# A decoder trunk with expert retrieval: PE's 16 products ahead of its step of mixing in every turn

## The reference

```
h = rms_norm(x, norm_mix);  z = h @ w_in                 # 1024 -> 2564
mixed = [forgetting attention | dilated attention | differential attention | S5 scan with GLU]
x = x + mixed @ w_out
h = rms_norm(x, norm_ffn)
# PEER: 8 heads, each with 2 x 128 keys; q = h @ peer_wq
top 16 of each half, top 16 of the 256 sums, gate = softmax(best 16)
act = gelu(sum_d h[t,d] * u_tab[id]) * gate              # 128 experts a token
x = x + sum_k act[t,k] * v_tab[id]
```

## Time and profile before

| | |
|---|---|
| median of 3 runs | 1836.1 us |
| the profiled execution | 1842.02 us |
| its span, first to last instruction | 1839.1 us |
| granted TensorE clock, mean | 0.905 |
| busy: PE / DVE / POOL / ACT | 1493.1 / 1157.0 / 1082.8 / 389.9 us |
| products of rows of v (L1112) | 2048 instructions, 982.4 us busy, 636 ns each |
| dot products (L865) | 512, 627.4 us busy, 1225 ns each |
| moved by DMA | 649.87 MB, of which 536.94 MB are gathers |

### The profile page before, as it was taken

The page is one execution under the profiler, slowest core; times in us unless marked ns, Lnnn a source line. Parts: engine busy times, 40 slices in busy tenths (PEclk is TensorE's granted clock), DMA queues, the critical chain, the costliest instruction groups (busy, mean ns, idle before and its releaser), DMA issues.

```text
span 1839.1 us, 15963 instructions
## 1 busy us (share of the span) xinstructions
PE 1493.1 (81%) x4780; PEld 799.9 (43%) x4780; DVE 1157.0 (63%) x2646; ACT 389.9 (21%) x991; POOL 1082.8 (59%) x1028
## 2 busy tenths in 40 slices
PE   6758379889898589889998579879998778777777
PEld 3546235445474234445464234445455433232332
DVE  6644954867469943877468933876648965445453
ACT  2221012233221121233221111233221121111111
POOL 0000345767666655777666655666766667777774
PEclk9768789989998889988999889999998988999889
DMA  7415589989999999999999999999999989999997
GB/s 307 160 35 207 204 359 380 399 297 363 373 401 408 340 418 409 405 369 385 374 401 408 336 415 351 395 340 331 374 376 405 369 301 410 409 409 409 407 388 307
DMA packets 179053, 649.87 MB, mean 353 GB/s; under 512 B 17783, under 2 KB 19319, under 8 KB 174105
## 3 DMA queue, kind: packets, MB, share of 16 engines
q0 software_dynamic: 147456, 536.94, 76.0%
q1 hardware_dynamic: 31512, 111.92, 15.7%
HBM read 644.07 MB, written 4.72 MB: 353 GB/s over the span
## 4 chain that ended last, share of the span: by engine, by line
PE 41%; DVE 32%; DMA 13%; issue 8%; POOL 4%; ACT 2%; DVEq 0%; SPq 0%; POOLq 0%
PE ps L1112 21%; DVE junk L865 12%; DMA ring_u<-table_u,ids 11%; PE ps L934 8%; PE ps L1069 3%; POOL ring_v L1143 2%; PE ps L1082 2%; DMA ring_v<-table_v,ids 1%; PE ps L999 1%; POOL ring_u L1138 1%; DVE W L690 1%; DVE W L842 1%; DVE W L844 1%; DVE W L845 1%; PE ps L1009 1%
## 5 line engine op out<-in xcount | busy, mean ns | idle before, releaser
L1112 PE MATMUL ps<-ring_v,diag 128*128 128x512 f32 x2048 | 982.4, 636 | 229.2 <-ACT diag L480 227.6
L865 DVE CUSTOM_DVE_ANT_0 junk<-ring_u,h 128x1024 bf16<-128x1024 f32 x512 | 627.4, 1225 | 268.1 <-DMA ring_u<-table_u,ids 212.5
L1138 POOL DMA_INDIRECT ring_u<-table_u,ids x512 | 536.1, 1047 | 387.7 <-DVE ids L849 204.9
L1143 POOL DMA_INDIRECT ring_v<-table_v,ids x512 | 546.5, 1067 | 352.2 <-PE ps L1112 269.9
L1112 PEld LDWEIGHTS ps<-ring_v,diag 128*128 128x128 f32 x2048 | 412.0, 205 | 761.4 <-issue 751.6
L471 ACT ACTIVATE acts<-dots 128x4 f32<-128x4 f32 x128 | 26.3, 205 | 998.6 <-DVE dots L865 998.6
L480 ACT ACTIVATE diag<-cst,weights 128x128 f32<-128x128 f32 x512 | 163.5, 390 | 39.2 <-DVE weights L874 39.0
L934 PE MATMUL ps<-W,hT 128*128 128x384 f32 (+2 forms) x384 | 142.9, 531 | 4.0 <-DVE hT L576 2.6
L1082 PE MATMUL ps<-hT,W 128*128 128x128 f32 x1024 | 117.7, 276 | 2.7 <-DVE hT L576 2.6
L1082 PEld LDWEIGHTS ps<-hT,W 128*128 128x128 f32 x1024 | 116.0, 192 | 3.8 <-DVE hT L576 3.8
L934 PEld LDWEIGHTS ps<-W,hT 128*128 128x128 f32 x384 | 73.7, 193 | 72.3 <-issue 36.9
(11 more groups left out here) (247 smaller groups left out, 1050.4 us busy)
## 6 DMA issues: line engine op xcount, KB each, us to landing
W<-w_in SPq DMA_DIRECT2D x32, 1282.0 KB, 15.2
W<-peer_wq SPq DMA_DIRECT2D x16, 2048.0 KB, 21.0
W<-w_out SPq DMA_DIRECT2D x4, 4096.0 KB, 19.5
ring_u<-table_u,ids POOLq DMA_INDIRECT x512, 7.8
ring_v<-table_v,ids POOLq DMA_INDIRECT x512, 7.7
W<-keys_t SPq DMA_DIRECT2D x4, 1024.0 KB, 8.3
zkv<-gain_mix SPq DMA_DIRECT2D x4, 512.0 KB, 16.0
toep<-ring_u SPq DMA_DIRECT2D x1, 2048.0 KB, 7.4
```

The costliest lines, as they stand in the source:

```text
L865: v.tensor_tensor_reduce(junk[:, :], ring_u[:, s, :], h[:, b, :], 1.0, 0.0, ALU.mult, ALU.add, dots[:, s:s + 1]).then_inc(dots_done, 1)
L1112: mm = pe.matmul(ps[:, c, :], diag[:, s, :], ring_v[:, s, c * 512:(c + 1) * 512], start=False, stop=False, skip_group_check=True)
L1138: gp.indirect_dma_start(ring_u[:, k % RING, :], None, table_u, bass.IndirectOffsetOnAxis(ap=ids[:, b, k:k + 1], axis=0)).then_inc(u_in[k % ...
L1143: gp.indirect_dma_start(ring_v[:, k % RING, :], None, table_v, bass.IndirectOffsetOnAxis(ap=ids[:, b, k:k + 1], axis=0)).then_inc(v_in[k % ...
```

## The change

The plan of a turn had the entry `rows of v` behind the step of mixing, but for the steps that begin with a norm (turns 0 and 20), where it stood ahead of it. Now it stands ahead of the step in every turn. The entry concerns PE alone; the order of the other engines is not touched.

```diff
             plan.append(("weigh", n, i))
 
-            late = not (left and left[0][0].startswith("norm"))
-            if not late:
-                plan.append(("rows of v", n, i))
+            plan.append(("rows of v", n, i))
             do(left[:1], n + 1)
             left = left[1:]
-            if late:
-                plan.append(("rows of v", n, i))
     plan.append(("gathered", PASSES - 1, 0))
```

## The result

| | before | after |
|---|---|---|
| median | 1835.6 us (1829.4 to 1840.6, 4 runs) | 2352.9 us (2347.3 to 2354.6, 4 runs) |
| ratio, 95% interval | | 1.2815, 1.277 to 1.286 |
| span of the profiled execution | 1839.1 us | 2344.4 us |
| granted clock, mean | 0.905 | 0.830 |
| L1112, now L1108: busy, mean | 982.4 us, 636 ns | 1087.1 us, 692 ns |

The page of the changed kernel, the chain that ended last, by engine and by line.

What follows compares the result with a forecast made beforehand. No single engine bounds it: the chain alternates, PE 41%, DVE 32%, transfers 13%. Profiled 1842 + 408 for the order + 105 for the clock = 2355, so median 2350 us; range 2220 to 2480.

Steps and rivals of the forecast that it cites:

- V: The 16 products of a turn on PE (L1112) that add rows of v; 7.0 us at the full clock.
- The file: Where DVE's mixing part needs M: dot products, V, M, DVE's part run in sequence, 13.4 us before M can start.
- the sum: First pass, dot products of turn 1 to those of turn 28: 489.7 us against 351.7, +138 us.
- The copy on ACT: Turns 21 and 22: ACT's copy of query 0 delays the Gelu, V starts at 22.3; together 35.7 us.
- The clock term: Three mixing passes: PE's work newly in sequence 18% slower at a lower clock, 35 us a pass, +105 us.
- M: PE's part of the mixing step in a turn; after the change it waits for V.
- The project turns: Turns 1 to 4: PE saturated in both orders, only 13.6 us added to 56.1, 69.7 us a pass.
- The rotation: Rival: PE's order only rotates, so just each pass's start pays, 13.6 us three times; 1880 us, chance 0.06.
- The floor of 397 us: Transfer limit of a mixing pass; rival: earlier V frees ring_v and passes reach it, 1768 us, chance 0.03.
- The high end of the clock: Rival: clock falls for good, every product takes twice the time, V near 14 us; 2800 us, chance 0.08.
- half of the file: Rival: something hides half of the +408 us put in sequence; about 2150 us, chance 0.07.
- the order's 408 us: Three mixing passes at full clock: +138 us for first and third, about +132 for second, +408 in all.

Runs made afterwards that it cites:

- PE kept at work: Changed kernel plus products with a zero matrix on PE filling the whole idle stretch until the next V, from turn 5 on: 2279.0 us, ratio 1.1924.
- their run: Kernel before with the products of rows of v moved ahead of the mixing step in turns 1 to 4 alone: 1883.3 us, ratio 1.0244.
- the kernel before with half of V: Kernel before with 8 instructions in place of 16 for the products of rows of v, second half of the columns not added: 1786.8 us, ratio 0.9712.
- the four runs with before at 1910 and 1917 us: Zero products in PE's idle stretches: changed kernel twice, 2279.0 and 2279.1 us; kernel before in two variants, 1899.7 and 1904.4 us.

## Why the prediction was right

It gave 2350 us and the median is 2352.9. Step by step, for the first pass (turns as there; the middle column is the changed kernel with PE kept at work, at the full clock but for V of turns 1 and 5, which took 9.01 and 9.32 us in place of 7.03):

| turns | predicted, full clock | measured, PE kept at work | measured, changed kernel |
|---|---|---|---|
| 1 to 4 | 69.7 | 71.1 | 71.6 |
| 5 | 19.8 | 21.8 | 22.1 |
| 8 | 29.7 | 29.7 | 31.1 |
| 10 | 19.3 | 19.3 | 21.6 |
| 13 | 15.8 | 15.7 | 17.2 |
| 16, 17 | 30.4 | 29.4 | 31.9 |
| 18, 19 | 37.4 | 37.6 | 40.1 |
| 21, 22 | 35.7 | 36.0 | 37.4 |
| 26, 27 | 39.8 | 39.6 | 44.1 |

*The file.* From D of turn 1 (253.57) to D of turn 28 (774.76) the changed kernel took 521.2 us; the sum was 489.7 and 35 for the clock. Over the same stretches of the three passes the kernel with PE kept at work lies 415 us above before, 402 without the slow V of turns 1 and 5, where 408 were worked out; the remaining turns gave back 9, which makes the 406 of the tables. What made this possible is that each turn is a sequence with one order in it, of durations that all stood in the trace before.

*The copy on ACT.* The prediction let the Gelu of turn 22 stand behind ACT's copy of query 0. The timeline of the changed kernel has it, ACT first and then DVE:

```profile
662.92 0.60 ACT L455 ACTIVATE W<-ps 128x512 f32<-128x512 f32 x1 [15.37 <-PE ps L1078]
663.41 0.20 ACT L467 ACTIVATE acts<-dots 128x4 f32<-128x4 f32 x1
...
663.64 0.16 DVE L870 TENSOR_TENSOR weights<-acts,gates 128x4 f32<-128x4 f32 x1 [12.05 <-ACT acts L467]
```

The dot products of the turn had ended at 651.6, and the weights waited 12.05 us. An engine that neither the diff nor the argument on PE and DVE names holds the turn up.

*The clock term* came out right in size, 105 against 101 to 114, but not in its make-up, so its closeness is luck in part. The prediction slowed V and M alike by 18%. In fact M isn't slowed behind V: query products took 276 ns before and after, project products 531 and 530, and those of the logits even went from 382 to 357 (L999, now L995), since before it was at times M that came first after a rest and met the low clock (rows below). V pays, mostly 8.5 to 10.0 us in place of 7.0, some 25%, since now it is what comes first. 19 V by 1.75 us is 33 us a pass. A kernel with longer M would have been misjudged.

*The project turns* cost 44 us by the median of their run (37 to 52 by its interval), with 41 worked out from 13.6 a pass (6.4 and 7.0 are 13.4). In that run's own trace turns 1 to 4 take 71.6, 72.0 and 72.0 us, and 56.1, 54.1 and 56.1 before, 49 us more. The missing 8 are mostly V of turn 1, which now comes first after a rest: 9.96 us in the second and third pass in place of 7.03 behind M. The sum had it at 7.0.

*The rivals.* The rotation holds for four turns. The floor of 397 us is real, but the new order goes away from it. The high end of the clock, V near 14 us, didn't come: the longest V was 10.2 us. Nothing hid half of the file. Of what the prediction wanted to see, L1108 with 31% of the chain, the clock of 0.82, 20 us for a turn of scores (21.5 with the clock) and the last pass at 10.24 us are there; transfers move 266, 276 and 264 GB/s where about 275 was given. Of the waits for PE's lines only part came as said: those for L1092 (now L1088) grew from 35.1 to 135.4 us, those for L1009 (L1005) doubled, those for L1069 (L1065) stayed at 50, and the longest, 31.2 us, is for the project line L930, which wasn't named.

That the median came within 3 us of the forecast is luck in part as well, since single terms are off by 6 to 9 us and cancel. That the order's 408 us came out at 402 isn't.

## What to carry to other kernels

Where two engines hand work back and forth, an engine's queue should hold the part that another engine waits for ahead of the bulk that only needs inputs: bulk placed first puts its own length and its inputs' wait on the other engine's path, here 13.4 us in 19 turns. Work the price out turn by turn from three numbers of the trace, when the moved block can start, its length, and what of the waiting engine's part needs the block behind it; turns where nothing needs it cost nothing. Ask last which products start each new stretch of PE after a rest, for those meet the low clock.

## What the runs showed of the hardware

Where V in the mixing passes of before and after came 3.4 to 15.3 us after the last product, the granted clock was 0.5 (1.2 GHz) for the first part of it, and its 16 products took 1.5 to 3.2 us longer together, never by all of the 7 that half the clock throughout would cost. V of turn 10 in the changed kernel, after 7.74 us of rest; the last columns are the clock, the share of DMA and GB/s:

```profile
437.76:442.40 4.64, 4.64 (x6) 2.06 (x7) 0.00 (x0) 0.74 (x3) 1.55 (x2) 0.51 0.87 275
442.60:447.10 4.50, 4.50 (x13) 2.01 (x12) 0.00 (x0) 0.00 (x0) 2.00 (x3) 1.00 0.76 222
```

After a rest of about 1 us V took 7.1 us, after 2.10 us either 8.80 or 7.10. Whatever comes first pays, and where that is short, so does what stands behind it. In turn 14 of the kernel before, M came first after 3.87 us of rest in the first pass and in the third; its products ran at full speed in the one, and at half speed at first in the other:

```profile
430.06 0.65 PE L1023 MATMUL ps<-cst,W 128*128 128x128 f32 x4 [3.87 <-DVE W L731]
430.55 0.60 PE L999 MATMUL ps<-W 128*128 128x256 f32 x2
...
1274.56 1.09 PE L1023 MATMUL ps<-cst,W 128*128 128x128 f32 x4 [3.87 <-DVE W L731]
1275.45 1.06 PE L999 MATMUL ps<-W 128*128 128x256 f32 x2
```

In the kernel before with half of V, the 16 products of the output projection that came first in turn 18 took 10.04 us in place of 7.0:

```profile
459.70 10.04 PE L1069 MATMUL ps<-W,hT 128*128 128x512 f32 x16 [3.98 <-issue]
```

In the kernel before, V of turn 11 stood behind 0.9 us of short products that came after 2.99 us of rest, and took 8.51 us, with the clock at 0.67 over its first 4.5 us. Filling the rest with products of zeros brought about 101 us in the changed kernel and 0.4 to 0.7% in the one before. The Trainium skill (TensorE: Matmul & The Clock Gate, "HAM oscillation — how this bites in real kernels") has bursts start throttled when waits recur; the trace agrees for the start of a burst, and shows that in a burst as long as V and M together the rest of it is spared (clock 1.00 from 442.60 on).

Chips differ: gathers of 4 KB rows with transfers as the bound moved 404 and 409 GB/s in the last pass of before and after, and 363 to 367 on the chips of the four runs with before at 1910 and 1917 us; elsewhere that kernel took 1836 to 1842.
